# Making the low part of each half weight tile on POOL in two instructions of 512 elements instead of one of 1024

## The reference

```python
# first block (256 tokens, D = 2048, D_FF = 8192)
hl = rmsnorm(x, norm1_w) * (1 + sc1) + sh1
x = x + g1 * token_mixer(hl, ...)                       # w_in, long convolution, state-space scan, w_out
hl2 = rmsnorm(x, norm2_w) * (1 + sc2) + sh2
x = x + g2 * (square(relu(hl2 @ w_mlp1)) @ w_mlp2)      # 2048 -> 8192 -> 2048
x = rmsnorm(x, final_norm_w)
# second block
proj = rms_norm(x, g_mix) @ w_in_2                      # retention, dilated attention, two gates
x = x + (sigmoid(gate_ret) * (ret @ w_br_ret) + sigmoid(gate_dil) * (dil @ w_br_dil)) @ w_out_2
x = x + memory_cross_attention(rms_norm(x, g_cross), rms_norm(mem, g_mem), w_q, w_kv, w_o)
# expert layer: 16384 experts, 16 chosen for each of 8 heads and each token
a = gelu(rms_norm(x, g_ffn) @ u_tab.T) * gates          # gates is zero for experts not chosen
x = x + a @ v_tab
out = rms_norm(x, g_final)
```

## Time and profile before

| | before |
|---|---|
| time, median of 3 runs | 4621.17 us (4618.63 to 4629.1) |
| time of the profiled execution | 4627.06 us |
| its span, first to last instruction | 4625.2 us |
| mean granted TensorE clock (share of full speed) | 0.968 |
| PE busy with matrix products | 4356.6 us, 94% of the span |
| DVE busy | 2626.7 us, 57% |
| ACT busy | 1718.1 us, 37% |
| POOL busy | 3298.1 us, 71% |
| DMA, mean over the span | 174 GB/s |

### The profile page before, as it was taken

How to read it: one execution, slowest core, us unless ns; L and a number is a source line. 1 busy time by engine, 2 the same in 40 slices (tenths; PEclk the granted TensorE clock), 3 DMA queues, 4 the chain that set the end, 5 groups by cost and what they waited for, 6 DMA issues and landing times.

```text
span 4625.2 us, 65525 instructions
## 1 busy us (share of the span) xinstructions
PE 4356.6 (94%) x24622; PEld 3660.4 (79%) x24622; DVE 2626.7 (57%) x3812; ACT 1718.1 (37%) x1868; POOL 3298.1 (71%) x1312
## 2 busy tenths in 40 slices
PE   8998989899999999999988998999999899899997
PEld 1676756788888878888877886899888788788876
DVE  3326775455445664643254312698867847875784
ACT  1234422433333343434434432443334333333433
POOL 0357740688888877877866884887887787788775
PEclk9999979999999999999999999999999999999999
DMA  8356750445555544445544552444554454454443
GB/s 315 130 200 248 298 193 15 170 172 189 178 185 182 178 158 158 177 164 182 188 149 146 186 186 92 168 168 166 180 180 169 164 183 173 155 186 178 165 169 121
DMA packets 111127, 805.21 MB, mean 174 GB/s; under 512 B 12903, under 2 KB 13192, under 8 KB 14088
## 3 DMA queue, kind: packets, MB, share of 16 engines
q1 hardware_dynamic: 108720, 787.30, 47.2%
q10 hardware_dynamic: 2200, 14.90, 0.9%
HBM read 800.06 MB, written 2.10 MB: 173 GB/s over the span
## 4 chain that ended last, share of the span: by engine, by line
PE 52%; POOL 17%; issue 10%; DVE 10%; ACT 1%; POOLq 0%; DMA 0%; DVEq 0%; ACTq 0%
PE psum L510 29%; POOL w_lo L435 16%; PE psum L512 14%; DVE out_hl L2852 2%; PE psum L638 2%; DVE out_hl L2850 1%; DVE hid L2848 1%; PE psum L1200 1%; PE psum L499 1%; PE psum L500 1%; PE psum L501 1%; PE psum L791 1%; PE psum L779 1%; DVE mix_m L2087 0%; DVE hid_hl L2334 0%
## 5 line engine op out<-in xcount | busy, mean ns | idle before, releaser
L435 POOL TENSOR_TENSOR w_lo<-ring,w_hi 128x1024 fp32r<-128x1024 f32 x1208 | 2928.2, 2427 | 1025.9 <-ACT w_hi L1276 1024.8
L1276 ACT ACTIVATE w_hi<-ring 128x1024 fp32r<-128x1024 f32 x1232 | 1302.3, 1060 | 2150.4 <-PE psum L512 1888.7
L510 PE MATMUL psum<-hc_hl,w_hi 128*128 128x512 f32 x5120 | 1835.9, 402 | 57.2 <-POOL w_lo L435 15.5
L512 PE MATMUL psum<-hc_hl,w_lo 128*128 128x256 f32 x5120 | 1436.0, 280 | 0.0
L510 PEld LDWEIGHTS psum<-hc_hl,w_hi 128*128 128x128 f32 x5120 | 968.3, 189 | 293.9 <-issue 32.0
L512 PEld LDWEIGHTS psum<-hc_hl,w_lo 128*128 128x128 f32 x5120 | 972.6, 190 | 4.9 <-issue 4.8
L510 PE MATMUL psum<-out_hl,w_hi 128*128 128x512 f32 x2048 | 726.4, 399 | 32.0 <-DVE x L2862 28.6
L512 PE MATMUL psum<-out_hl,w_lo 128*128 128x256 f32 x2048 | 576.6, 282 | 0.0
L510 PEld LDWEIGHTS psum<-out_hl,w_hi 128*128 128x128 f32 x2048 | 388.5, 190 | 126.4 <-DVE x L2862 29.5
L512 PEld LDWEIGHTS psum<-out_hl,w_lo 128*128 128x128 f32 x2048 | 390.7, 191 | 0.0
L510 PE MATMUL psum<-hid_hl,w_hi 128*128 128x512 f32 x1024 | 367.9, 403 | 16.9 <-DVE hid_hl L2336 12.4
(11 more groups left out here) (454 smaller groups left out, 5576.5 us busy)
## 6 DMA issues: line engine op xcount, KB each, us to landing
ring<-stream SPq DMA_DIRECT2D x652, 1024.0 KB, 4.8
ring<-mixed SPq DMA_DIRECT2D x96, 1024.0 KB, 6.8
x<-x ACTq DMA_DIRECT2D x2, 2048.0 KB, 11.1
ctx_raw<-ctx ACTq DMA_DIRECT2D x1, 2048.0 KB, 9.5
mem_raw<-mem ACTq DMA_DIRECT2D x1, 2048.0 KB, 9.2
out<-x SPq DMA_DIRECT2D x4, 512.0 KB, 2.7
filt_w<-filt_w ACTq DMA_DIRECT2D x1, 1024.0 KB, 11.3
dft<-dft ACTq DMA_DIRECT2D x1, 1024.0 KB, 13.1
```

The costliest lines, as they stand in the source:

```text
L435: pool.tensor_tensor(w_lo[:, slot], ring[:, s, k], w_hi[:, slot].bitcast(F32), ALU.subtract).then_inc(lo_ready, 1)
L510: pe.matmul(psum[:, b, :].rearrange("p (s t) -> p s t", s=2), w_hi[:, slot, c], x_hl, start=start(c), stop=False, skip_group_check=True)
L512: m = pe.matmul(psum[:, b, 0:T], w_lo[:, slot, c], x_hl[:, 0], start=False, stop=stop(c), skip_group_check=True)
L1276: act.activation(w_hi[:, 2 * (s % 2) + h], ring[:, s, k], ACT.Copy).then_inc(hi_ready, 1)
```

## The change

The one subtraction over 8 blocks (1024 elements) becomes a loop of two over 4 blocks each (512 elements), written to the two halves of the same place of `w_lo`. POOL waits before the first as before; only the second counts `lo_ready` up. Nothing else in the kernel is touched: L463, L470, L479, L441 and L448 stay as they are.

```diff
                     for h in range(2):
                         pool.wait_ge(hi_ready, i * 8 + (hi0 + 2 * s + h + 1))
-                        k = slice(h * KC // 2, (h + 1) * KC // 2)
                         slot = 2 * (s % 2) + h
-                        pool.tensor_tensor(w_lo[:, slot], ring[:, s, k], w_hi[:, slot].bitcast(F32),
-                                           ALU.subtract).then_inc(lo_ready, 1)
+                        for c in range(0, KC // 2, 4):
+                            m = pool.tensor_tensor(w_lo[:, slot, c:c + 4], ring[:, s, h * KC // 2 + c:h * KC // 2 + c + 4],
+                                                   w_hi[:, slot, c:c + 4].bitcast(F32), ALU.subtract)
+                        m.then_inc(lo_ready, 1)
```

## The result

| | before | after |
|---|---|---|
| median of four runs each | 4625.14 us (4618.63 to 4632.0) | 4587.85 us (4585.86 to 4595.0) |
| span of the profiled execution | 4625.2 us | 4586.7 us |
| mean granted TensorE clock | 0.968 | 0.971 |
| DVE busy | 2626.7 us | 2584.7 us |
| POOL busy | 3298.1 us | 3504.4 us |

The ratio is 0.9922 (95% interval 0.9902 to 0.9942): 36 us faster, between 27 and 45. So the direction was right and the size was wrong.

The account below looks back on a forecast made before the run. PE bounds the normal state and DVE, held by POOL's subtractions, the turns. Terms -14.4, -2.4, -3.6, +0.4, +1.7 and +2.0 sum to -16.3 us, from the median 4621.17 to 4605 us; range 4595 to 4638.

Parts of the forecast that it names:

- The cost on POOL: POOL's split subtraction: 1.34 us a piece, 2.64 a pair, 0.24 more than now, hidden under PE's 2.77 per half.
- The boundary inside a pair: Between POOL's two pieces a held DVE operation gets its turn, so it takes 1.42 us instead of 2.47.
- The first rival: POOL starts its second piece before DVE gets in; held operations wait 2.64 us, not 2.40: 4642 us, chance 0.10.
- Gain 1: Turn from up to down in three expert quarters: PE's stall for `sum_out` shrinks 4.8 us each, -14.4 us.
- Gain 2: Last MLP group: DVE keeps up with PE and its last operation comes earlier, -2.4 us.
- Gain 3: Three norms where PE waits for a held last multiply-subtract: half a subtraction each, -3.6 us.
- The seven MLP groups: The other MLP groups: PE's 1.78 us wait for the last hidden tile stays, +0.05 us each, +0.4 us.
- Losses: Waits and restarts where POOL is the last link, +1.7 us, and POOL's stretch without a pause, +2 us.
- the stretch of the earlier trace: Where POOL runs 16 halves without a pause: between 0 and 3.8 us lost, +2 us taken.
- The rival of no change: Each let-in DVE operation delays POOL by its whole 0.43 us, eating the gain: about 4619 us; chance 0.28 with similar cases.

Follow-up runs that it names:

- mid_two: Two pieces only from the retention branch to the product keys, against the kernel before: 4620.02 us, ratio 0.9986.
- turn_late_two: Two pieces only for the first four down tiles of each expert quarter, against the kernel before: 4608.3 us, ratio 0.9969.
- turn_early_two: Two pieces only for the last eight up tiles of each expert quarter, against the kernel before: 4616.28 us, ratio 0.998.
- four_pieces: Four pieces of 256 elements for every half, against the kernel before with one subtraction of 1024: 4696.31 us, ratio 1.0143.
- three_pieces: Three pieces of 384, 384 and 256 elements for every half, against the kernel before: 4600.39 us, ratio 0.9941.
- psum_both_two: Two pieces everywhere and the hidden tiles of expert layer and MLP in PSUM, against the kernel before: 4539.84 us, ratio 0.9821.
- psum_hidden_two: Two pieces everywhere and the expert layer's hidden tile in PSUM, against the kernel before: 4567.87 us, ratio 0.9884.
- peer_two: Two pieces only in the expert layer, one instruction elsewhere, against the kernel before: 4599.46 us, ratio 0.9936.

## Why the prediction was wrong, by its own steps

**The cost on POOL: right.** Forecast 1.34 for a piece and 2.64 for a pair; 1.32 in the mean over all. Undisturbed it is less: 1.293 us (the durations above), and 2.54 for a pair in POOL's timeline. From 1.293 and the earlier trace rows's 2.396 the fixed part is 0.19 us, not 0.27: the line through 1024 and 2048 elements was drawn from two different lines of the kernel and overstated it. Each DVE operation let in costs POOL more than the 0.06 us that I took from the earlier trace rows: four pieces with three operations let in take 5.46 us, where four undisturbed ones take some 5.04 (twice 2.54 less an overlap), so 0.14 each. The two errors cancel. The estimate from the Trainium skill (GPSIMD Engine Reference, "Elementwise — side-by-side cycle accounting") gave 0.06 us fixed and 2.46 for a pair; the measured 2.54 lies between it and mine.

**The boundary inside a pair: right for the turn, too broad as a rule.** DVE gets in, at 1.26 to 1.46 us (forecast 1.42). But "DVE gets its turn at each boundary" doesn't hold everywhere: the multiply of 2048 elements let a boundary pass in the trace of before already (6.56 us), and eight in `mid_two`. The first rival is out where PE waited in after, not as a mechanism.

**Gain 1, the wait for `sum_out`: right in size.** Forecast -14.4 us, measured -14.1.

**Gain 1, what it left out: the step that failed.** I worked the turn from the bank sum at 3616.24 us on, and looked only at the wait behind it. But the backlog of DVE begins at 3586, and where DVE is the bound, PE pays for each period, not only at the end: with two banks it waits for the bank sum. The row was there (9.5 us in six waits) and I didn't read it. `turn_late_two` and `turn_early_two` show the two halves apart, 14 and 9 us. Together with the clock behind these stalls (-2.6) the three turns gave 23.6 us in the trace, not 14.4: 9.2 us more.

**The clock: not in the sum.** The prediction priced each stall by its length. Behind a stall the clock may fall, as the traces show, for 1.2 to 2.3 us of lost time. The stalls that went or shrank gave back about 5.9 us. Another 5.9 us lie behind four MLP stalls that are nearly as long in after; executions of the same code differ by as much, and how much of it is the change is open.

**Gain 2: right.** -2.4 forecast; the waits of the last group fell from 4.6 to 2.1 us, the clock gave 1.2, and 1.7 of that stage's 5.4 us are PE's pace.

**Gain 3: about right.** -3.6 forecast. The norms' waits are 2.5 us shorter (L1823: 14.8 to 13.5, one of 1.8 us gone, L2351 longer by 0.6).

**The seven MLP groups: right.** 1.78 us became 1.65. The waits fell by 1.0 us together, from 12.4 to 11.4, and not by 0.4 the other way. The rest of the 10.6 us in the stage table is the clock behind four stalls (5.9), the norm before the MLP (its wait 1.1 less, the clock behind it 1.4), some 0.8 of PE's pace in the first group, and 0.4 that I can't name.

**Losses: too high.** +3.7 forecast. The waits for POOL grew by 1.1 us, and the stretch of the earlier trace rows lost nothing in the profile of after (-0.4 us), though 6 us in `mid_two`, by the DVE instruction that was shut out. The far end of that term wasn't 3.8 us for POOL's own cost; it was a DVE instruction that loses its turn, in `four_pieces` for up to 30 us.

Of the 22.2 us between the forecast and the difference of the two spans (38.5), the bank waits are 5.8, the clock behind stalls that shrank 5.9, the clock behind four MLP stalls 5.9, the losses 2.6 and the MLP groups' waits 1.4; 0.6 is left. This is the account of one pair of profiles, and the clock behind the four MLP stalls may belong in part or whole to the executions that were profiled. **The range** was too narrow on the fast side: its far end was built from terms that were in the sum, and half of the miss (5.8 and 5.9 of 22.2 us) came from waits and clock time that were not in it.

**The rival of no change** put the let-in operation's whole 0.43 us on POOL. The trace shows 0.14 each. The rule of the Trainium skill behind it (SBUF — State Buffer, "Who interferes with whom": who comes second "fully blocks") agrees with the held operations, which end behind POOL's piece; what a let-in operation costs POOL it doesn't say, and here it is a third of that operation's time.

## What to carry to other kernels

Where one engine is behind over a stretch, add up every wait for it in that stretch, for every buffer that it frees, before pricing a change of its pace; the longest stall alone gave little more than half. Cutting a long instruction of an engine that shuts another one out is cheap only while the cuts hide under the bound and that engine still pauses (two pieces won 36 us, three 27, four lost 66): without pauses it can shut the other out for tens of microseconds. The best remedy was no cut at all: moving the operand that causes the hold to PSUM gave 64 us with whole subtractions. And before a difference between two profiles is explained, look for the same stretch in further executions: here some 6 us of 38 were a clock that falls in one execution and not in another, and equal code ran at two paces that differ by 2%.

## What the runs showed of the hardware that I had not expected

A DVE instruction that waits for POOL doesn't always get the next boundary: the 128x2048 multiply at 1894.57 us in `mid_two` let eight pass in 10 us, and its like took 13.2 us in `three_pieces` and 14.1 in `four_pieces`, while it took 2.3 in after and `psum_both_two`. In the kernels with one instruction of 1024 elements there it took 4.1 to 6.6. Of the six kernels with pieces there, three (after, `psum_hidden_two`, `psum_both_two`) got it through at once. It isn't a matter of long operations: ones of 256 elements were shut out for 12.77 us in `psum_hidden_two` and for up to 28.72 us in `four_pieces`. Most of the long ones got through only at the next pause of POOL. What decides stays open.

At full granted clock the products run at one of two paces, 0.347 or 0.353 us from one with `w_hi` to the next, and equal code has the one in one execution and the other in another. `peer_two` against after in the MLP shows it, at 176.3 and 173.6 ns for a product.

A DVE subtraction with one input in PSUM and one in SBUF takes 0.42 us beside POOL, and so does a cast from PSUM, without exception in the 128 instructions of each in the expert layer.
